# Merging three attention branches: the first four output blocks of a projection taken piece by piece over eight PSUM banks

## What is computed

```python
def gla_output(o, r, g_o, w_o):
    ...
    return (o * jax.nn.silu(r)) @ w_o

def merge(gate_logits, y_gla, y_swa, y_mem, w_out):
    g = jax.nn.sigmoid(gate_logits.astype(jnp.float32)).astype(y_gla.dtype)
    g1, g2, g3 = jnp.split(g, 3, axis=-1)
    return (g1 * y_gla + g2 * y_swa + g3 * y_mem) @ w_out
```

## Time and profile before

| what | value |
|---|---|
| median of 3 runs | 5435.06 us (5430.29 to 5442.83) |
| the profiled execution's own time | 5435.13 us |
| its span in the trace | 5433.3 us |
| PE busy over the span | 5161.4 us, 95% |
| POOL busy over the span | 3489.8 us, 64% |
| DVE busy over the span | 2467.3 us, 45% |
| stage_merge, PE's first to last matmul | 2191.1 to 2387.3 us |
| PE's first matmul of the stage after it | 2401.6 us |

### The profile page before, as it was taken

How to read it: one execution, slowest core, us unless ns; L and a number is a source line. 1 busy time by engine, 2 the same in 40 slices (tenths; PEclk the granted TensorE clock), 3 DMA queues, 4 the chain that set the end, 5 groups by cost and what they waited for, 6 DMA issues and landing times. The chain is left out here.

```text
span 5433.3 us, 90535 instructions
## 1 busy us (share of the span) xinstructions
PE 5161.4 (95%) x33434; PEld 5007.2 (92%) x33434; DVE 2467.3 (45%) x3782; ACT 830.0 (15%) x1318; POOL 3489.8 (64%) x2072
## 2 busy tenths in 40 slices
PE   8899999999999889989999999999998899999998
PEld 8899999999989776989898889999998899999998
DVE  1200000012211243430207777888885788888854
ACT  2100000023322333100101111212211000000001
POOL 7555555544444232555456777888887799999974
PEclk9999999999999989999999999999999999999999
DMA  5333333333232443652323334988897888888852
GB/s 195 130 113 110 109 111 110 117 105 108 83 122 101 146 149 113 214 179 82 119 105 131 122 126 147 327 322 323 323 334 258 318 309 301 311 308 301 301 170 95
DMA packets 344224, 1011.39 MB, mean 186 GB/s; under 512 B 39632, under 2 KB 133680, under 8 KB 308288
## 3 DMA queue, kind: packets, MB, share of 16 engines
q1 hardware_dynamic: 162992, 524.56, 28.6%
q0 software_dynamic: 36864, 268.45, 12.9%
q10 hardware_dynamic: 144176, 215.86, 11.2%
HBM read 883.11 MB, written 126.76 MB: 186 GB/s over the span
## 5 line engine op out<-in xcount | busy, mean ns | idle before, releaser
L208 POOL TENSOR_TENSOR w_lo<-w_raw,w_hi 128x1024 fp32r<-128x1024 f32 x906 | 2216.9, 2447 | 168.5 <-POOL w_hi L204 167.2
L204 POOL TENSOR_SCALAR w_hi<-w_raw 128x1024 fp32r<-128x1024 f32 x906 | 1003.7, 1108 | 1676.2 <-PE ps L232 1453.5
L228 PE MATMUL ps<-h_hi,w_hi 128*128 128x272 f32 (+1 forms) x6816 | 1740.8, 312 | 85.2 <-DVE h_lo L321 34.5
L232 PE MATMUL ps<-h_hi,w_lo 128*128 128x272 f32 (+1 forms) x6816 | 1718.2, 309 | 0.0
L230 PE MATMUL ps<-h_lo,w_hi 128*128 128x272 f32 (+1 forms) x6816 | 1708.3, 308 | 0.0
L228 PEld LDWEIGHTS ps<-h_hi,w_hi 128*128 128x128 f32 x6816 | 1144.4, 190 | 111.1 <-issue 105.4
L230 PEld LDWEIGHTS ps<-h_lo,w_hi 128*128 128x128 f32 x6816 | 1144.1, 190 | 6.4
L232 PEld LDWEIGHTS ps<-h_hi,w_lo 128*128 128x128 f32 x6816 | 1138.0, 190 | 2.8
L228 PE MATMUL ps<-ex_c_hi,w_hi 128*128 128x416 f32 x2048 | 720.0, 352 | 34.8 <-DVE ex_c_lo L2345 34.5
L232 PE MATMUL ps<-ex_c_hi,w_lo 128*128 128x416 f32 x2048 | 723.7, 353 | 0.0
L230 PE MATMUL ps<-ex_c_lo,w_hi 128*128 128x416 f32 x2048 | 715.7, 349 | 0.0
(11 more groups left out here) (260 smaller groups left out, 4621.5 us busy)
## 6 DMA issues: line engine op xcount, KB each, us to landing
w_raw<-weights SPq DMA_DIRECT2D x906, 512.0 KB, 3.3
up<-up_out ACTq DMA_DIRECT2D x128, 208.0 KB, 3.3
gate<-g_sb_g ACTq DMA_DIRECT2D x13, 2048.0 KB
ex_up<-up ACTq DMA_DIRECT2D x32, 832.0 KB, 7.9
ex_gate<-gate ACTq DMA_DIRECT2D x32, 832.0 KB, 12.7
proj<-in_stage ACTq DMA_DIRECT2D x73, 272.0 KB, 2.1
br_gate<-proj ACTq DMA_DIRECT2D x48, 272.0 KB, 3.3
branches<-gla_beside ACTq DMA_DIRECT2D x32, 272.0 KB, 2.3
```

The lines of the kernel that those rows point to most:

```text
L204: pool.tensor_scalar(self.whi[:, slot, :], self.raw[:, slot, :], 1.0, 1.0, ALU.mult, ALU.mult).then_inc(self.hi_done, 1)
L208: pool.tensor_tensor(self.wlo[:, slot, :], self.raw[:, slot, :], self.whi[:, slot, :].bitcast(F32), ALU.subtract).then_inc(self.split_done, 1)
L228: pe.matmul(acc, hi, x, start=first, stop=False)
L232: mm = pe.matmul(acc, lo, x, start=False, stop=last)
```

## The change

PE's order changes for the first four blocks: the first pieces of blocks 0, 1, 2 and 3, then their second pieces, each block in its own pair of PSUM banks (all eight banks). From block 4 on the order is as before, first and second piece of one block, now over four pairs, so that PE waits for `y0` of block j - 4. PE's and DVE's loops become straight code; ACT's loop stays, and so do SP's and POOL's lists, since the eight pieces are reordered in the array on the host. DVE waits for `piece_of(j, 1) + 1`.

```diff
+        piece_of = lambda j, piece: AT_GLA_OUT + (4 * piece + j if j < 4 else 2 * j + piece)
...
         @block.tensor
         def _(pe):
-            def body(q):
-                for u in range(2):
-                    j = 2 * q + u
-                    if needed(q):
-                        pe.wait_ge(dve_s.sem, dve_s.at("y0", j - 2))
-                        held(pe)
-                    for piece in range(2):
-                        starts = isinstance(j, int) and j == 0
-                        core.use_piece(pe, (AT_GLA_OUT + 2 * u + piece) % RING, 4 * q + (AT_GLA_OUT + 2 * u + piece), [
-                            (core.acc(u), parts(hi, k), parts(lo, k), k == 0, k == KD - 1,
-                             (load.lo_ready, k + 1) if starts else None, None)
-                            for k in range(PIECE_K * piece, PIECE_K * (piece + 1))])
-            rounds(pe, KD // 2, body)
+            def one(j, piece):
+                if piece == 0 and j >= 4:
+                    pe.wait_ge(dve_s.sem, dve_s.at("y0", j - 4))
+                i = piece_of(j, piece)
+                core.use_piece(pe, i % RING, i, [
+                    (core.acc(j % 4), parts(hi, k), parts(lo, k), k == 0, k == KD - 1,
+                     (load.lo_ready, k + 1) if j == 0 else None, None)
+                    for k in range(PIECE_K * piece, PIECE_K * (piece + 1))])
+            for piece in range(2):
+                for j in range(4):
+                    one(j, piece)
+            for j in range(4, KD):
+                one(j, 0)
+                one(j, 1)
...
             def body(q):
-                for u in range(2):
-                    j = 2 * q + u
+                for u in range(4):
+                    j = 4 * q + u
...
-                    dve.wait_ge(core.piece_used, 2 * j + (AT_GLA_OUT + 2))
+                    dve.wait_ge(core.piece_used, piece_of(j, 1) + 1)
...
-            rounds(dve, KD // 2, body)
+            for q in range(KD // 4):
+                body(q)
...
+    gla = out[AT_GLA_OUT:AT_GLA_OUT + 8]
+    gla[:] = gla.reshape(4, 2, P, PIECE_K, P).transpose(1, 0, 2, 3, 4).reshape(8, P, PIECE_K, P).copy()
```

## The result

The changed kernel took 5455.84 us (median of 8 runs, 5446.69 to 5464.21) against 5438.26 us for the kernel before (8 runs beside it): a ratio of 1.0024, 95% interval 1.0014 to 1.0033, or 13.1 us more (7.6 to 18). The two medians by themselves lie further apart, 17.6 us; the text goes by the ratio, and gives both where it matters. A second set of runs gave 1.0022 (1.0014 to 1.0031), and medians 12.7 us apart. Forecast were +9.7 us, 5444.8 in a range of 5435 to 5453; the measured ratio, applied to the 5435.13 us on which the forecast was built, gives 5448.2, and the 17.6 us would give 5452.7.

A forecast was written before the change was run, and what follows sets the result against it. The stage was taken to end with the transfer and copy chain, not PE: 13.5 us later at block 0, less what turns of 12.3 and a freer end give back, +9.7 us, so 5444.8 us, range 5435 to 5453.

The forecast's parts named there:

- The bound: Stage end: set by the chain of transfers, `y1`, `y2`, `y0`, sums and ACT's copy, in which PE has no part.
- Start: PE's wait for the first low activation chunk: unchanged by the new order, gain 0.
- Block 0: Block 0 ends with PE's fifth piece, so `y0` and the whole chain start 13.5 us later; first copy at 2228.5.
- +2.4 for its first sums: Written sum's entry for block 0's sums meeting POOL's `w_lo`: +2.4 us.
- Turns: Distance between successive ACT copies: 12.3 us each, between 12.0 and 12.68; thirteen turns, 159.9 us.
- The lock: GpSimd and two-input VectorE operations exclude each other, so the chain could not outrun PE's pace while POOL splits.
- Free turns: Last two turns, after POOL's splits end: 10.8 us into block 14, then 9.9.
- Sum: Whole stage: copy of block 15 at 2409.1 against 2399.36, +9.7 us.
- Straight code, four pairs, next stage: Unrolled PE and DVE code, four bank pairs and the next stage's start after a longer gap: each worth 0.
- The Trainium skill's rule on taken branches: Straight code gains because a taken branch can force a fetch and stall; 5434.8 us, chance 0.02.
- The third rival: Slower still: more late transfers or PE held by code fetch; turns of 12.9 give +16.5, 5451.6 us; chance 0.28.
- rivals 1 and 2: Chain catches up: faster, turns at 10.7 or below, 5424.7 us, chance 0.04; or loss caught, 5434 to 5439, chance 0.14.

The follow-up runs named there:

- cuts: Changed kernel with POOL's `w_lo` split on 64 of 1024 columns, 28 weight transfers at 32 KB, or both: 0.9995, 1.0015, 0.9982 of before.
- early issue: ACT issues the five transfers of block j + 1 ahead of its copy of block j: changed kernel 0.9965 of before, kernel before 0.9960.
- N = 1: Changed kernel with only its order undone, first blocks one after the other, straight code and four bank pairs kept: 1.0001 of before.
- thin `w_lo`: Changed kernel with POOL's second split of this stage's weight pieces made on 64 of 1024 columns: 0.9995 of before.

## Why the prediction was right, and where its sizes were off

- **The bound.** Right: the stage ends with the chain of ACT's copies, not with PE, and PE's last matmul came 1.4 us sooner than before (194.8 for 196.2) and only lengthened the gap.
- **Start.** Right: 0. PE's entry for the low chunks is 11.1 us for 11.2.
- **Block 0.** `y0` forecast 32.4 us after PE's first matmul (2223.5 less 2191.1), measured 32.6. First copy forecast 37.4, measured 37.4; the sums took 3.81 us, under a `w_lo`, as in the row of block 12 that I chose. One entry of the written sum is wrong: "+2.4 for its first sums" sets block 12's 5.02 us from `y0` to copy against block 15's 2.66, but block 0 of before took 3.41 (2210.00 to 2213.41), so the difference is 1.6. The places, and with them the +9.7, do not use it.
- **Turns.** The term that was mis-sized. I set 12.3 between 12.0 and 12.68, since two turns of 15 us might hold by chance. Thirteen turns were 167.75 us, 12.90 each, outside the upper bound, and worth +7.8 us against the sum. The three traces of before have 12.60, 12.80 and 13.15 for the same thirteen turns, so 12.90 is no more than this chain has anyway, and the upper bound from one trace was too low by half a microsecond. Turns of 14.5 us and more are in all nine traces of the kernels without cuts and without early issue; in before and in the changed kernel they come with late landings. They are not rare.
- **The lock.** Wrong in its general form: "the chain could not outrun PE's pace while POOL splits". With early issue it did, in turns of 7.6 to 9.1 us under full splits. It made no difference to the sum, as the turns of this kernel stayed above 12.
- **Free turns.** 10.66 for 10.8 and 10.98 for 9.9: +0.9 us. There were three, not two: the chain was so late that the turn into block 13 was free as well, 10.55, and the twelve before it had a mean of 13.10.
- **Sum.** Copy of block 15 forecast 218.0 us after PE's first matmul, measured 226.8, so the profiled stage grew by 18.5 and not 9.7, and the gap before the next stage was 34.2 us and not 24. The time grew by 13.1 (17.6 by the medians), because the first trace of before was at the short end too: against the three (208.3, 212.2 and 216.2, mean 212.2) the copy of block 15 is 14.6 later. The short turns of one trace went into the turns of the forecast and into its starting point, and the two errors cancel in part. That the time came out so near the forecast is in that part luck; the cause, a chain that starts 13.5 us later and gives little back, is not.
- **Straight code, four pairs, next stage.** No cost that can be measured, as said; 1.0001 (0.9990 to 1.0011) with the order undone. PE's first pair of the next stage takes 0.79 us as before. The Trainium skill's rule on taken branches ("Runtime: NRT & Kernel Launch", "Instruction fetch mechanics") was a rival; the order in loops came out at 1.0038 and in straight code at 1.0024 and 1.0022, and the intervals overlap, so no run here settles a gain.
- **Rivals.** The measured +13.1 us lies at the upper end of the forecast's own +5 to +13.7. The third rival, turns of 12.9 us, had the size of the turns right and with it a price of +16.5; the short first trace makes the difference. The catching up of rivals 1 and 2 needed turns under 11.7 on average; with full splits and transfers, and these behind the copy, no trace had a mean under 12.7 over the first twelve turns or under 12.3 over all fifteen.
- **Left open.** Why the last turns without POOL are 10.0 to 11.3 us and not always 9.88. Whether four pairs of banks lengthen the turns a little. And in the profile the stage of N = 1 was 8 us longer than the first one of before, while the times were the same; the third trace of before explains it by spread, but one trace each does not prove it.

## What to carry to other kernels

An engine that is 95% busy can still not be what ends a stage: compare its last instruction with the end, and look for a chain through other engines whose turn is longer than that engine's period. To finish the first blocks later in order to keep that engine fed shifts such a chain by the delay less the slack that it had (18 us less 4.7 here), and the chain gives nothing back while its turn is the longer one. Take the latency out of the turn first, here by issuing the next transfers before the wait; then the order of the first blocks stops mattering. And a mean over turns that collide with transfers needs more than one profiled execution before it carries a sum.

## What the runs showed of the hardware that was not expected

- A queue's transfers can take longer beside another's: the 272 KB of a branch landed after 3.8 us beside a 32 KB weight transfer and after 7.2 us beside 512 KB ones (medians of two), in one kernel, ten microseconds apart. The gates' transfers, of the same size and issued just before, took 2.8 us both times, and in the uncut kernels most turns have 3.9 to 4.9 us beside 512 KB transfers too.
- DVE waiting for POOL can do more than add time; it can lock a chain to POOL's work. With small weight transfers nine turns had a mean of 11.98 us, two weight pieces of PE, though the turn took 10.76 with the thin `w_lo`. A shorter turn is not held so: with early issue, under full splits, turns were 7.6 to 9.1 us.
